# Two-layer encoder trunk: the second mixer's heads in a new order of steps, with VectorE adding the fourth sum of weight quarters

## The chip, the cores and the metric

The kernel runs on one core of a Trainium2 chip. The metric is device time in microseconds (us) for one execution of the whole program, from its start to its end.

## The reference, cut to what matters

The program is an encoder trunk of two layers on 256 rows of 2048 features, all in float32. Layer 1 mixes with differential attention, layer 2 with gated linear attention; each is followed by a squared-ReLU MLP of 8192 hidden features and has residual connections and layer norms. The change lies in the second mixer:

```python
def gla(x, w_in, w_gk2, b_gk, g_norm, w_o):
    proj = x @ w_in                       # q, k: 4 heads x 256; v, r: 4 heads x 512; z: 16
    q, k, v, r, z = jnp.split(proj, [...], axis=-1)
    log_a = jax.nn.log_sigmoid(z @ w_gk2 + b_gk) / 16
    ...                                   # b = cumsum of log_a in each chunk of 64 rows
    attn = jnp.where(causal, (q * exp(b)) @ (k * exp(-b)).T, 0)
    o = attn @ v + (terms of earlier chunks)
    o = rms_norm(o, g_norm) * silu(r)
    return o @ w_o
```

## The kernel before, in words

**Products in three parts.** TensorE multiplies in float32r. To keep float32 accuracy, each weight tile is split in two: ScalarE copies `raw` into a rounded `hi`, and VectorE subtracts, `lo = raw - hi`. Activations `X` lie ready as two such parts too. Each product is then three groups of matmuls: high part times `hi`, low part times `hi`, high part times `lo`. A weight tile is 128 partitions by 4 x 512 numbers (1 MB). `hi` has four slots, `lo` three; the semaphores `hi_ready`, `lo_ready` and `w_used` count tiles, and a slot is written again once the tile that lay there is used.

**The four heads.** After q and k of all heads (groups `G_GLA` to `G_GLA + 3`), a loop over four heads computes v and r (512 columns each, 16 blocks of 128 input features, in four "quarters" 0 to 3). Quarters 0 and 1 of v and r, for two row blocks, would be eight products; a Strassen-like scheme makes seven of them, `p0` to `p6`, from sums of weight quarters and from sums of activations (`gla_form`, forms S1 to S4, made once). Quarters 2 and 3 are plain tiles: `v2`, `v3`, `r2`, `r3`. A product is 12 matmuls, a plain tile 24. `HEAD_AT` fixes the order on TensorE: p0, p1, p3, p2, p5, p4, v2, p6, v3, r2, r3. Between them `key_pairs` makes the score maps of the head (24 small matmuls), `weigh_gla` multiplies them with v (9), and `turn_gla` transposes the output of the head before.

**Sums of weight quarters.** Four sums are needed in a head. `head_sum(h, 1)` and `head_sum(h, 2)` are made by VectorE in place in the raw slot of role 0 (for p1 and p2). The third (`head_sums(h, 3)`, for p4) and the fourth (`head_sums(h, 4)`, for p6) are transfers that accumulate, issued on GpSimd's queue: they read a quarter from HBM and add it to what lies in the slot. Each waits until the tile's last reader is through.

**What else goes on.** Of the head before: `r_total` (VectorE) ends r, `sigmoid_block` (ScalarE) and `gate_r` (VectorE) make silu(r), `gain_r` (GpSimd) multiplies by the norm's gain, `norm_gla` (VectorE) scales the output, `o_hi_gla` and `o_lo_gla` split it. Of this head: `keep` (ScalarE) copies a finished product from PSUM, so that p2, p5 and p4 can go on in its bank (`product_kept`), `r_difference` and `split_v` (VectorE) combine them. Each engine has its instructions in one written order, so that an instruction that waits holds up all behind it. SyncE issues the plain loads in written order too; the load of `v2` goes to the raw slot that held v's quarter 1 (role 3: p3's tile, and an operand of `head_sum(h, 2)`), and waits for `lo` of p3. The loads of v3, r2 and r3 wait for `lo` of p5, p4 and p6.

**Head 0.** VectorE also makes the key tensors there, `gla_k(0)` for heads 0 and 1 and `gla_k(1)` for heads 2 and 3. Both used one buffer `gla_qk`, so the k sums of group `G_GLA + 3` waited until `gla_k(0)` was done.

**After the heads.** `rows_late` is the first output group of the mixer (also used for the first mixer's).

Of the kernel before, what the change touches and what calls it, by code (L numbers as in the profile page):

```python
# [32 lines left out]
D = 2048  # L33
# [82 lines left out]
FORM_LO = {S1: 1, S2: 2, S3: 3, S4: 4}  # L116
BANK = 4
# [3 lines left out]
def build(nc, x, attn_w_qkv, attn_w_o, attn_lambda, attn_subln, gla_w_in, gla_w_gk2, gla_b_gk,  # L121
          gla_norm, gla_w_o, mlp_w1, mlp_w2, ln_g, ln_b, out):
    ctx = ExitStack()
    with ctx:
# [95 lines left out]
        gla_qk = part(3072, 2, 2, SEQ)  # L220
# [113 lines left out]
        gla4_added = sem("gla4_added")  # L334
# [53 lines left out]
        def _(sp):  # L388
# [122 lines left out]
            for h in range(GLA_HEADS):  # L511
# [3 lines left out]
                sp.wait_ge(lo_ready, at + HEAD_AT["p3"])  # L515
                load_head(h, HEAD_RAW["v2"], 2, v)
# [24 lines left out]
        def _(pool):  # L541
# [79 lines left out]
            def head_sums(h, n):  # L621

                a = HEAD_TILES * h + 4 * G_VR
                if n == 3:
                    pool.wait_ge(gla_summed, 2 * h + 1)
                    c = 2 * KEY + D + COLS * h
                    pool.dma_start(raw[:, head_slot(h, 1)], w_in[:, KPT:2 * KPT, c:c + COLS], accum_op=ALU.add
                                   ).then_inc(gla3_added, 16)
                else:
                    pool.wait_ge(lo_ready, a + HEAD_AT["p2"] + 1)  # L630
                    c = 2 * KEY + COLS * h
                    pool.dma_start(raw[:, head_slot(h, 0)], w_in[:, KPT:2 * KPT, c:c + COLS], accum_op=ALU.add
                                   ).then_inc(gla4_added, 16)
# [9 lines left out]
            def gain_r(h):  # L643
                for t in range(TB):
                    pool.wait_ge(r_gated, 2 * h + t + 1)
                    pool.tensor_tensor(silu_r[:, t, :], silu_r[:, t, :], gla_gain, ALU.mult).then_inc(r_gained, 1)

            head_sums(0, 3)
# [12 lines left out]
            gain_r(GLA_HEADS - 1)  # L661
# [12 lines left out]
        def _(pe):  # L674
# [22 lines left out]
            def rows_late(g, acts, ready, bank_free, after=None):  # L697


                for t, tiles in ((0, (0, 1, 2)), (1, (0, 1, 2)), (0, (3,)), (1, (3,))):  # L700
                    for j in tiles:
                        if j == 0:
                            pe.wait_ge(*bank_free[t])
                        if t == 0:
                            pe.wait_ge(lo_ready, 4 * g + j + 1)
                            pe.wait_ge(*ready(j))
                        acc = ps[:, 4 * t, :]
                        for k in range(KPT):
                            a = 4 * j + k
                            mm(acc, acts[:, a, 0, blk(t)], hi[:, j, k, :], a == 0, False)  # L710
                            mm(acc, acts[:, a, 0, blk(t)], lo[:, j, k, :], False, False)
                            m = mm(acc, acts[:, a, 1, blk(t)], hi[:, j, k, :], False, a == KT - 1)
# [512 lines left out]

            def head(h):
# [14 lines left out]
                pe.wait_ge(form_lo, FORMED_GLA + FORM_LO[S1])  # L1241
# [3 lines left out]
                pe.wait_ge(form_lo, FORMED_GLA + FORM_LO[S2])  # L1245
# [18 lines left out]
            for h in range(GLA_HEADS):  # L1264
# [3 lines left out]
                (0, 2): lambda: turn_gla(h, 0), (1, 0): lambda: turn_gla(h, 1)})  # L1268
# [7 lines left out]
        def _(act):  # L1276
# [356 lines left out]
            def head_hi(h, name):  # L1633
# [3 lines left out]
                if name in ("p1", "p2"):  # L1637
                    act.wait_ge(gla_summed, 2 * h + int(name[1]))
                elif name == "p4":
                    act.wait_ge(gla3_added, 16 * h + 16)  # L1640
                elif name == "p6":
                    act.wait_ge(gla4_added, 16 * h + 16)
# [43 lines left out]
            def head_squares(h):  # L1686
                act.wait_ge(go_done, h + 1)
                for t in range(TB):
# [5 lines left out]
            head_form_high(S1)  # L1694
            head_hi(0, "p1")
            for h in range(GLA_HEADS):
                if h == 0:
                    act.wait_ge(w_used, 4 * G_VR)
                    head_form_high(S3)
                    head_form_high(S2)  # L1700
                    head_form_high(S4)
                    copy_halves(G_GLA + 3, COLS_GLA + 3, 1, gla_half)
                    head_hi(0, "p3")
# [8 lines left out]
                keep(h, "p2", 0, silu_r[:, 0, :], (go_normed, 2 * h - 1) if h else (key_step, 8 * GLA_HEADS))  # L1712
                head_hi(h, "v2")
                if h:
                    o_hi_gla(h - 1, 0)
                    o_hi_gla(h - 1, 1)
                copy_pairs(h)
                head_hi(h, "p6")
                head_hi(h, "v3")
                head_hi(h, "r2")  # L1720
                head_hi(h, "r3")
                v_high(h)
                if h + 1 < GLA_HEADS:
                    head_hi(h + 1, "p0")
                    head_hi(h + 1, "p1")
                    head_squares(h)
                    head_hi(h + 1, "p3")
                else:
                    split_hi(G_GWO, 0, G_GWO - AHEAD_GWO)
                    split_hi(G_GWO, 1, G_GWO - AHEAD_GWO)  # L1730
# [877 lines left out]
```

## Time and profile before

| what | value |
|---|---|
| median of 3 runs | 2150.2 us (2144.88 to 2152.44) |
| the profiled execution | 2147.14 us |
| its span in the trace | 2145.4 us |
| TensorE busy | 2115.8 us, 99% |
| VectorE, ScalarE, GpSimd busy | 1751.6, 1195.7, 187.0 us |
| mean granted TensorE clock | 0.994 |

In the span TensorE is busy nearly throughout. Matmuls are pipelined: a 128x512 one has a duration of 0.39 us, but the next starts 0.227 us behind it, so that spacing, and not duration, tells the pace. "Idle before" is the time that an engine stood still ahead of an instruction, and the arrow names what released it.

### The profile page before, as it was taken

What the parts mean: (1) busy time and instruction counts of PE and PEld (TensorE: products, weight loads), DVE (VectorE), ACT (ScalarE), POOL (GpSimd) and SP (SyncE); (2) the same over time, 40 slices, a digit from 0 to 9 for tenths busy, and PEclk for the clock granted to TensorE, in tenths of its full rate; (3) what the DMA queues carried; (4) which work ended last, traced back from release to release, by engine and by line L of the source; (5) the groups of instructions that cost most, each with busy time, mean ns of one, the idle gap of its engine ahead of it and who ended that gap; (6) DMA issues with size and microseconds to landing.
All of it is one profiled execution on the core that took longest, in us unless ns stands there. A gap on an engine that the chain in (4) does not pass through costs nothing.

```text
span 2145.4 us, 27042 instructions
## 1 busy us (share of the span) xinstructions
PE 2115.8 (99%) x10922; PEld 1811.0 (84%) x10922; DVE 1751.6 (82%) x1489; ACT 1195.7 (56%) x1066; POOL 187.0 (9%) x155
## 2 busy tenths in 40 slices
PE   9999999999999999999999999999999999999998
PEld 8888888988888888888887777889888888888886
DVE  5555559888998998988878667698889989989887
ACT  5444445556666656656474555545566666566562
POOL 3000000300000000000110111103000000000000
PEclk9999999999999999999999999999999999999999
DMA  9445547578988988888655666775788888888884
GB/s 316 166 150 201 173 148 246 201 230 239 263 254 250 259 244 279 243 231 252 225 185 165 187 196 197 250 237 201 230 239 262 255 250 259 244 278 244 231 253 155
DMA packets 241761, 487.37 MB, mean 227 GB/s; under 512 B 7856, under 2 KB 7856, under 8 KB 240624
## 3 DMA queue, kind: packets, MB, share of 16 engines
q1 hardware_dynamic: 204928, 406.61, 53.4%
q0 software_dynamic: 36288, 78.39, 19.8%
q8 instruction: 80, 1.31, 0.2%
q10 hardware_dynamic: 432, 0.79, 0.1%
q14 instruction: 33, 0.27, 0.0%
HBM read 483.66 MB, written 2.10 MB: 226 GB/s over the span
## 4 chain that ended last, share of the span: by engine, by line
PE 93%; DVE 3%; ACT 1%; issue 1%; DMA 1%; POOL 0%; ACTq 0%; DVEq 0%
PE ps L676 57%; PE ps L1002 8%; PE ps L1000 8%; PE ps L1006 8%; PE ps L880 2%; PE ps L937 1%; PE ps L942 1%; PE ps L935 1%; PE ps L1215 1%; PE ps L1222 1%; PE ps L1217 1%; DMA raw<-in_gla_w_in_dram 1%; ACT hi L1646 1%; DVE lo L2413 1%; PE ps L747 1%
## 5 line engine op out<-in xcount | busy, mean ns | idle before, releaser
L676 PE MATMUL ps<-X,hi 128*128 128x512 f32 (+1 forms) x3008 | 697.2, 377 | 2.7 <-ACT work L1601 1.2
L676 PEld LDWEIGHTS ps<-X,hi 128*128 128x128 f32 x3008 | 549.2, 188 | 102.7 <-ACT work L1601 1.4
L1484 ACT ACTIVATE hi<-raw 128x2048 fp32r<-128x2048 f32 x196 | 372.6, 1915 | 236.3 <-DVE raw L2145 152.0
L2131 DVE TENSOR_TENSOR lo<-raw,hi 128x2048 fp32r<-128x2048 f32 x196 | 444.7, 2286 | 20.0 <-PE ps L1006 10.8
L676 PE MATMUL ps<-X,lo 128*128 128x256 f32 x2816 | 387.0, 283 | 0.0
L676 PEld LDWEIGHTS ps<-X,lo 128*128 128x128 f32 x2816 | 373.2, 191 | 12.8
L1750 DVE TENSOR_TENSOR lo<-raw,hi 128x2048 fp32r<-128x2048 f32 x104 | 237.7, 2296 | 106.7 <-ACT hi L1282 104.9
L1282 ACT ACTIVATE hi<-raw 128x2048 fp32r<-128x2048 f32 x119 | 226.3, 1914 | 157.5 <-PE ps L676 117.4
L2131 DVE TENSOR_TENSOR lo<-up_raw,hi 128x2048 fp32r<-128x2048 f32 x112 | 256.0, 2286 | 32.3 <-PE ps L676 32.3
L1468 ACT ACTIVATE hi<-up_raw 128x2048 fp32r<-128x2048 f32 x112 | 214.2, 1912 | 22.1 <-PE ps L1006 11.2
L1000 PE MATMUL ps<-hi,forms 128*128 128x512 f32 x448 | 175.3, 391 | 0.4 <-issue 0.4
L1002 PE MATMUL ps<-hi,forms 128*128 128x512 f32 x448 | 175.5, 392 | 0.0
L2156 DVE TENSOR_TENSOR res<-res,ps 128x512 f32<-128x512 f32 x196 | 131.3, 682 | 49.7 <-PE ps L1006 49.5
L2413 DVE TENSOR_TENSOR lo<-raw,hi 128x2048 fp32r<-128x2048 f32 x44 | 99.6, 2288 | 43.7 <-ACT hi L1646 43.7
L2145 DVE TENSOR_TENSOR raw<-raw 128x2048 f32<-128x2048 f32 x56 | 127.9, 2284 | 0.0
L1006 PE MATMUL ps<-lo,forms 128*128 128x512 f32 x448 | 119.7, 389 | 0.0
L1646 ACT ACTIVATE hi<-raw 128x2048 fp32r<-128x2048 f32 x44 | 82.8, 1908 | 62.4 <-DMA raw<-in_gla_w_in_dram 30.0
L1495 ACT ACTIVATE work<-ps 128x512 f32<-128x512 f32 x64 | 34.7, 595 | 133.0 <-PE ps L676 133.0
L555 POOL DMA_DIRECT2D raw<-in_mlp_w_dram x28 | 36.1, 1290 | 739.7 <-DVE raw L2145 739.7
L1006 PEld LDWEIGHTS ps<-lo,forms 128*128 128x128 f32 x448 | 84.1, 188 | 17.4
L1000 PEld LDWEIGHTS ps<-hi,forms 128*128 128x128 f32 x448 | 84.5, 189 | 15.6 <-issue 0.7
L1002 PEld LDWEIGHTS ps<-hi,forms 128*128 128x128 f32 x448 | 84.5, 189 | 15.4
(278 smaller groups left out, 2860.3 us busy)
## 6 DMA issues: line engine op xcount, KB each, us to landing
raw<-in_mlp_w_dram SPq DMA_DIRECT2D x144, 1024.0 KB, 7.9
up_raw<-in_mlp_w_dram SPq DMA_DIRECT2D x112, 1024.0 KB, 7.7
raw<-in_mlp_w_dram POOLq DMA_DIRECT2D x56, 1024.0 KB, 9.2
raw<-in_gla_w_in_dram SPq DMA_DIRECT2D x48, 1024.0 KB, 5.5
raw<-in_attn_w_qkv_dram SPq DMA_DIRECT2D x47, 1024.0 KB, 5.1
raw<-in_attn_w_o_dram SPq DMA_DIRECT2D x16, 1024.0 KB, 6.4
raw<-in_gla_w_o_dram SPq DMA_DIRECT2D x16, 1024.0 KB, 6.4
raw<-in_gla_w_in_dram POOLq DMA_DIRECT2D x8, 1024.0 KB, 9.0
```

Of the source, the lines that this page charges most:

```text
L676: return pe.matmul(o, w, m, start=start, stop=stop)
L1000: pe.matmul(acc, a_hi, hi[:, at % 4, k, :], start=start and k == 0, stop=not start, skip_group_check=not start)
L1002: pe.matmul(acc, a_lo, hi[:, at % 4, k, :], start=False, stop=not start, skip_group_check=not start)
L1006: m = pe.matmul(acc, a_hi, lo[:, at % 3, k, :], start=False, stop=k == KPT - 1 or not start, skip_group_check=not start)
L1282: act.activation(hi[:, j], raw[:, j], ACT.Copy).then_inc(hi_ready, 1)
L1468: act.activation(hi[:, U_AT[j] % 4], up_raw[j % UP_SLOTS][:, :, :], ACT.Copy).then_inc(hi_ready, 1)
L1484: act.activation(hi[:, P_AT[p] % 4], raw[:, slot], ACT.Copy).then_inc(hi_ready, 2 if p == PRODUCTS - 1 else 1)
L1750: dve.tensor_tensor(lo[:, j], raw[:, j], hi[:, j].bitcast(F32), ALU.subtract).then_inc(lo_ready, 1)
L2131: dve.tensor_tensor(lo[:, at % 3], src, hi[:, at % 4].bitcast(F32), ALU.subtract).then_inc(lo_ready, n)
L2145: dve.tensor_tensor(raw[:, a], raw[:, a], raw[:, j], ALU.add).then_inc(t_summed, 1)
L2156: dve.tensor_tensor(d, d, ps[:, BANK + bank, :], op).then_inc(res_added, 1)
L2413: dve.tensor_tensor(lo[:, n % 3], raw[:, head_slot(h, HEAD_RAW[name])], hi[:, n % 4].bitcast(F32), ALU.subtract).then_inc(lo_ready, 1)
```

## The change

Four things:
1. The fourth sum of weight quarters is made by VectorE (`head_sum(h, 3)`: the raw slot of role 0 plus that of role 3, in which v's quarter 1 still lies), not by a transfer. So v2's load, which overwrites role 3, now waits for that sum as well.
2. The written orders on TensorE, ScalarE and VectorE change. VectorE's `head_sum(h, 2)` comes right behind `lo` of p1, in the head before; ScalarE splits p3 and p2 ahead of the sigmoids; `lo` of the next head's p0 comes between `v_total` and `split_v`. On TensorE the transposes of the head before come behind p4, both together; `key_pairs` comes behind p5 (in head 0 behind p4).
3. In head 0 `gla_qk` has a second buffer, and `gla_k(1)` is moved behind the split of v2, in two halves around the split of p6.
4. v2 and `rows_late` take the matmuls on `hi` first, row block by row block, and wait for `lo` only behind them (before: `rows_late` waited for `lo` at once).

```diff
@@ sync
                 sp.wait_ge(lo_ready, at + HEAD_AT["p3"])
+                sp.wait_ge(gla_summed, 3 * h + 3)
                 load_head(h, HEAD_RAW["v2"], 2, v)
@@ gpsimd
-                    gain_r(h - 1)
-                head_sums(h, 4)
+                    gain_r(h - 1, 0)
+                    gain_r(h - 1, 1)
                 mask_pairs(h)
                 if h + 1 < GLA_HEADS:
-                    head_sums(h + 1, 3)
+                    third_sum(h + 1)
                 gla_power(h)
@@ tensor, rows_late
                         if t == 0:
-                            pe.wait_ge(lo_ready, 4 * g + j + 1)
+                            pe.wait_ge(hi_ready, 4 * g + j + 1)
...
@@ tensor, head
                 head_product(h, "p2", 0, form(S2), False)
+                pe.wait_ge(product_kept, 3 * h + 2)
+                pe.wait_ge(form_lo, FORMED_GLA + GLA_LO[S4])
+                head_product(h, "p5", 1, form(S4), False)
+                if h:
+                    key_pairs(h)
+                pe.wait_ge(product_kept, 3 * h + 3)
+                pe.wait_ge(form_lo, FORMED_GLA + GLA_LO[S3])
+                head_product(h, "p4", 0, form(S3), False)
                 if h:
                     turn_gla(h - 1, 0)
-                pe.wait_ge(product_kept, 3 * h + 2)
-                pe.wait_ge(form_lo, FORMED_GLA + FORM_LO[S4])
-                head_product(h, "p5", 1, form(S4), False)
-                if h:
                     turn_gla(h - 1, 1)
-                key_pairs(h)
-                pe.wait_ge(product_kept, 3 * h + 3)
-                head_product(h, "p4", 0, form(S3), False)
-                head_tile(h, "v2", (3, 0), False, (r_differed, h + 1))
+                else:
+                    key_pairs(h)
+                head_tile_by_rows(h, "v2", (3, 0), (r_differed, h + 1))
@@ scalar
+            head_form_high(S2)
             head_hi(0, "p1")
+            head_hi(0, "p3")
             for h in range(GLA_HEADS):
...
                 else:
+                    head_hi(h, "p2")
                     sigmoid_block(h - 1, 0)
+                    keep(h, "p0", 0, first_kept[:, :], free)
                     sigmoid_block(h - 1, 1)
-                keep(h, "p0", 0, first_kept[:, :], (go_done, h) if h else None)
-                head_hi(h, "p2")
-                keep(h, "p1", 1, second_kept, (go_done, h) if h else None)
-                head_hi(h, "p5")
+                    head_hi(h, "p5")
+                keep(h, "p1", 1, second_kept, free)
                 head_hi(h, "p4")
@@ vector, heads 1 to 3
                     r_total(h - 1, 0)
                     head_lo(h, "p3")
                     r_total(h - 1, 1)
-                    head_sum(h, 2)
                     gate_r(h - 1, 0)
                     head_lo(h, "p2")
                     gate_r(h - 1, 1)
                     head_lo(h, "p5")
+                    head_sum(h, 3)
                     norm_gla(h - 1, 0)
                     norm_gla(h - 1, 1)
                     head_lo(h, "p4")
...
                 head_lo(h, "r3")
-                split_v(h)
+                v_total(h)
                 if h + 1 < GLA_HEADS:
                     head_lo(h + 1, "p0")
+                    split_v(h)
                     head_sum(h + 1, 1)
                     head_lo(h + 1, "p1")
+                    head_sum(h + 1, 2)
                     mean_squares(h)
```

## Rows read from the trace of the kernel before

**Rows 1.** The page's busy time of the engines over the whole span
```profile
PE 2115.8 (99%) x10922; PEld 1811.0 (84%) x10922; DVE 1751.6 (82%) x1489; ACT 1195.7 (56%) x1066; POOL 187.0 (9%) x155
```

**Rows 2.** Busy time by windows, one per head; columns: PE, PEld, DVE, ACT, POOL, PEclk, DMA
```profile
1160.62:1217.22 56.60, 50.98 (x215) 41.98 (x214) 42.02 (x41) 29.02 (x29) 3.61 (x4) 0.91 0.69 194
1217.22:1269.79 52.57, 48.83 (x222) 39.79 (x221) 36.20 (x28) 27.58 (x28) 8.23 (x6) 0.97 0.68 198
1269.79:1322.48 52.69, 48.76 (x222) 39.39 (x221) 36.64 (x28) 26.64 (x24) 8.22 (x6) 0.97 0.68 198
1322.48:1375.60 53.12, 49.83 (x223) 40.50 (x222) 34.92 (x28) 29.94 (x31) 7.59 (x6) 0.94 0.75 217
```

**Rows 3.** The waits of TensorE, whole span: total us, times, longest us
```profile
PE ps L1195 <- ACT hi L1646: 9.7, 4, 3.0
PE ps L1185 <- DVE work L2476: 3.8, 3, 2.3
PE ps L1201 <- DVE lo L2413: 2.9, 2, 2.7
```

**Rows 4.** Timeline of TensorE, end of head 0: start us, us, instruction
```profile
1209.74 0.39 PE L676 MATMUL ps<-gla_v_hi,pair_hi 128*128 128x512 f32 x1
...
1211.78 0.39 PE L1215 MATMUL ps<-hi,X 128*128 128x512 f32 x1
...
1217.22 0.39 PE L1195 MATMUL ps<-hi,X 128*128 128x512 f32 x1
```

**Rows 5.** Timeline of TensorE, heads 0 and 1, where it stalls and slows
```profile
1171.89 0.47 PE L1195 MATMUL ps<-hi,gla_form 128*128 128x512 f32 x1 [2.91 <-ACT hi L1646]
...
1174.04 0.63 PE L1195 MATMUL ps<-hi,gla_form 128*128 128x512 f32 x1
...
1181.00 1.19 PE L1201 MATMUL ps<-lo,gla_form 128*128 128x512 f32 x4 [2.71 <-DVE lo L2413]
...
1232.58 0.66 PE L1185 MATMUL ps<-ident,work 128*128 128x128 f32 x4 [2.27 <-DVE work L2476]
...
1237.84 2.79 PE L676 MATMUL ps<-G 128*128 128x64 f32 x24
1240.44 0.48 PE L1195 MATMUL ps<-hi,gla_form 128*128 128x512 f32 x1
```

**Rows 6.** Timeline of VectorE, head 0 and the start of head 1
```profile
1149.47 0.69 DVE L2393 TENSOR_TENSOR G<-G,work 128x512 f32<-128x512 f32 x1
...
1154.09 2.28 DVE L2413 TENSOR_TENSOR lo<-raw,hi 128x2048 fp32r<-128x2048 f32 x1
...
1192.03 6.69 DVE L2413 TENSOR_TENSOR lo<-raw,hi 128x2048 fp32r<-128x2048 f32 x3
...
1220.83 2.28 DVE L2421 TENSOR_TENSOR raw<-raw 128x2048 f32<-128x2048 f32 x1
```

**Rows 7.** Timeline of ScalarE: three splits in head 0, table load in head 1
```profile
1188.14 5.51 ACT L1646 ACTIVATE hi<-raw 128x2048 fp32r<-128x2048 f32 x3
...
1217.90 1.28 ACT L1668 ACT_TABLE_LOAD   x1
```

**Rows 8.** All GpSimd gains (line 646): duration ns min/median/max
```profile
L646 POOL TENSOR_TENSOR work<-work x8: 1266/2272/3272, 1223.9 to 1383.7; 128x512 f32<-128x512 f32 x8
```

**Rows 9.** Timelines of GpSimd and VectorE behind head 3: a gain beside two VectorE operations
```profile
1379.76 3.27 POOL L646 TENSOR_TENSOR work<-work 128x512 f32<-128x512 f32 x1 [7.35 <-DVE work L2469]
...
1381.80 1.78 DVE L2469 TENSOR_TENSOR work<-work 128x512 f32<-128x512 f32 x1
```

**Rows 10.** Transfers, from issue to landing: SyncE's plain loads (line 501)
```profile
DMA to landing us min/median/max: 4.9/5.6/10.8
```

**Rows 11.** The same for GpSimd's fourth sum (line 632)
```profile
DMA to landing us min/median/max: 8.4/11.9/12.5
```

**Rows 12.** Timeline of TensorE, head 2: a short stall and the matmul behind it
```profile
1286.22 0.66 PE L1185 MATMUL ps<-ident,work 128*128 128x128 f32 x4 [1.31 <-DVE work L2476]
...
1286.94 0.39 PE L1197 MATMUL ps<-hi,gla_form 128*128 128x512 f32 x1
```

More of the change, by code:

```diff
@@ L116 @@
 FORM_LO = {S1: 1, S2: 2, S3: 3, S4: 4}
+GLA_HI = {S1: 1, S2: 2, S3: 3, S4: 4}
+GLA_LO = {S1: 1, S2: 2, S4: 3, S3: 4}
 BANK = 4
@@ L641, in mask_pairs, with gain_r @@
                                    pattern=[[0, 2], [1, P]], channel_multiplier=-1).then_inc(pairs_masked, 1)
[L643 to L648, printed above, removed]
+            def gain_r(h, t):
+                pool.wait_ge(r_gated, 2 * h + t + 1)
+                pool.tensor_tensor(silu_r[:, t, :], silu_r[:, t, :], gla_gain, ALU.mult).then_inc(r_gained, 1)
+            third_sum(0)
             pool.wait_ge(form_lo, FORMED_GLA + 4)
@@ L710, in rows_late @@
                             mm(acc, acts[:, a, 0, blk(t)], hi[:, j, k, :], a == 0, False)
-                            mm(acc, acts[:, a, 0, blk(t)], lo[:, j, k, :], False, False)
-                            m = mm(acc, acts[:, a, 1, blk(t)], hi[:, j, k, :], False, a == KT - 1)
+                            mm(acc, acts[:, a, 1, blk(t)], hi[:, j, k, :], False, False)
+                        if t == 0:
+                            pe.wait_ge(lo_ready, 4 * g + j + 1)
+                        for k in range(KPT):
+                            a = 4 * j + k
+                            m = mm(acc, acts[:, a, 0, blk(t)], lo[:, j, k, :], False, a == KT - 1)
                         if t == 1:
@@ L1224, in head_tile, with head_tile_by_rows @@
                 m.then_inc(w_used, 1)
+            def head_tile_by_rows(h, name, banks, second_free):
+                n = HEAD_TILES * h + HEAD_AT[name]
+                a = KPT * int(name[1])
+                pe.wait_ge(hi_ready, 4 * G_VR + n + 1)
+                for t in range(TB):
+                    if t:
+                        pe.wait_ge(*second_free)
+                    for k in range(KPT):
+                        for part_of_x in range(2):
+                            pe.matmul(ps[:, banks[t], :], X[:, a + k, part_of_x, blk(t)], hi[:, n % 4, k, :], start=False,
+                                      stop=True, skip_group_check=True)
+                    if t == 0:
+                        pe.wait_ge(lo_ready, 4 * G_VR + n + 1)
+                    for k in range(KPT):
+                        m = pe.matmul(ps[:, banks[t], :], X[:, a + k, 0, blk(t)], lo[:, n % 3, k, :], start=False,
+                                      stop=True, skip_group_check=True)
+                m.then_inc(w_used, 1)
             def head(h):
@@ L2374, in gla_k_sums, with gla_k @@
                     b = 4 * (u % 2) + 2 * s
-                    dve.tensor_tensor(gla_qk[:, s], ps[:, b:b + 2, 0:SEQ], gla_half[:, s], ALU.add
+                    dve.tensor_tensor(gla_qk[u][:, s], ps[:, b:b + 2, 0:SEQ], gla_half[:, s], ALU.add
                                       ).then_inc(halves_added, 1)
-            def gla_k(u):
+            def gla_k(u, only=(0, 1)):
                 n = COLS_GLA + 2 + u
                 dve.wait_ge(decays_ready, 5)
-                for s in range(2):
+                for s in only:
                     h = 2 * u + s
@@ L2516, in _ @@
             gla_form_lo(S1)
-            gla_k(0)
             head_lo(0, "p0")
             head_sum(0, 1)
+            gla_form_lo(S2)
+            gla_k(0)
             head_lo(0, "p1")
+            head_sum(0, 2)
             for h in range(GLA_HEADS):
                 if h == 0:
-                    gla_form_lo(S2)
-                    gla_k_sums(1)
                     head_lo(0, "p3")
-                    head_sum(0, 2)
+                    head_lo(0, "p2")
+                    gla_form_lo(S4)
                     gla_form_lo(S3)
-                    gla_form_lo(S4)
-                    head_lo(0, "p2")
-                    gla_k(1)
+                    head_sum(0, 3)
                     head_lo(0, "p5")
                     head_lo(0, "p4")
+                    gla_k_sums(1)
+                    head_lo(0, "v2")
+                    r_difference(0)
+                    gla_k(1, (0,))
+                    head_lo(0, "p6")
+                    gla_k(1, (1,))
+                    head_lo(0, "v3")
+                    pairs_low(0)
+                    head_lo(0, "r2")
                 else:
```

83 lines of the change are left out of this document (42 added, 41 removed).

## The prediction

> **What bounds the kernel now.** I read the busy time of the page first: TensorE is at work 99% of the span [rows 1], so only what makes it stand or run slowly can be won. Then its waits over the whole program: nearly all that matter lie at three lines of the four heads, 9.7 + 3.8 + 2.9 = 16.4 us [rows 3]. Then windows, one for each head: 56.60, 52.57, 52.69 and, up to the first matmul of the output group, about 52.9 us, at a granted clock of 0.91 to 0.97 [rows 2]. That clock is the second loss.
>
> The least that a head can take comes from a stretch without stalls [rows 4]: a plain tile takes 5.44 us (1211.78 to 1217.22), so a product with half as many matmuls 2.72, and `weigh_gla` 2.04. `key_pairs` takes 2.60 (1237.84 to 1240.44) [rows 5], the two transposes about 0.9. So a head needs 7 x 2.72 + 4 x 5.44 + 2.04 + 2.60 = 45.4 us, and 46.3 with the transposes (heads 1 to 3). Above that lie 11.2, 6.3, 6.4 and 6.6 us: 30.5 us in all, the most that the change can bring here. The stalls are 16.4 of it; the rest is slow matmuls of 0.63 us, in place of 0.39, behind them [rows 5].
>
> **Why it stalls.** Before, VectorE makes `head_sum(h, 2)` 3.6 us into the head (1220.83 to 1223.11 in head 1, [rows 6]), ScalarE splits p2 only behind that and a sigmoid, and TensorE waits. In head 0 `gla_k(1)` (4.6 us, as `gla_k(0)` from 1149.47 to 1154.09, [rows 6]) stands ahead of the splits of p5 and p4: the 2.71 us stall. In heads 1 to 3 the transposes wait for `norm_gla` (2.27 us at the longest) [rows 5].
>
> **The prices.** A split or a sum on VectorE takes 2.28 us alone and 2.20 in a row (6.69 for three) [rows 6], a 512-wide operation 0.6; a split on ScalarE 1.8 in a row and 1.9 alone (5.51 for three, [rows 7]); a plain load 5.6 us to landing [rows 10]. T is a head's start on TensorE.
>
> **Part 1, head 0.** VectorE now does `lo` p0 at 1149.5, sum 1, form S2, `gla_k(0)` to 1159.1, `lo` p1 to 1161.4, sum 2 to 1163.6, `lo` p3, `lo` p2 to 1168.0. TensorE wants p2 at 1168.8, and its `lo` 1.8 us later: the 2.91 stall goes. Forms S4 and S3, sum 3 to 1171.4, `lo` p5 to 1173.6: p5 starts at 1171.5 and wants `lo` at 1173.3, so 0.25 us are lost. `lo` p4 (1175.8) is in time. v2's load goes at 1171.4, lands at 1177.0, `hi` at 1179.0, ahead of 1179.9 where TensorE comes to it. The halves of `gla_k(1)` (2.3 us each) delay `lo` of p6 and v3 to 1186.4 and 1190.9, needed at 1187.1 and 1191.6: hidden, with 0.7 us to spare. If that cover went, each later microsecond would be one of TensorE's. What comes late next is `weigh_gla`: r3's load waits for `lo` p6, so it lands at 1192.0; `hi`, `lo`, `v_total`, the next head's `lo` p0 (now ahead of `split_v`: 2.2 us that before did not stand there) and `split_v` end at 1200.3; TensorE is there at 1198.9: 1.4 us. Head 0 then takes 45.4 + 0.25 + 1.4 = 47.1 us, 9.5 less.
>
> **Part 2, heads 1 to 3.** `head_sum(h, 2)` ends about T + 0.6 (T + 1.2 in head 1), `hi` p2 at T + 2.6, far ahead of T + 8.2: that stall (9.7 us in all four heads, 3.0 at the longest, [rows 3]) goes. The transposes are wanted at T + 18.9 and the norms end before T + 16: that stall goes too. The new critical chain hangs on sum 3, since v2's load now waits for it, and SyncE's loads of v3 and r2 queue behind it. `r_total(0)`, `lo` p3, `r_total(1)`, `gate_r(0)`, `lo` p2, `gate_r(1)`, `lo` p5, sum 3: with the sigmoid between, sum 3 ends at T + 12.0 (12.9 in head 1, whose first sigmoid has a table load of 1.28 us ahead, [rows 7]).
>
> That is if nobody disturbs VectorE. The eight gains on GpSimd take from 1.27 us, with VectorE at rest, to 3.27, started beside a split [rows 8]. In the one place where a VectorE operation with both inputs in SBUF follows, it was 1.78 us in place of the usual 0.7, while the gain ran its 3.27 us [rows 9]. In the new order `gate_r(1)` stands so behind `lo` p2 and sum 3 behind `lo` p5, each with a gain waiting. I price each at the measured 1.1 us: 2.2 us, sum 3 at T + 14.2 (15.1 in head 1). The bounds: 0, since the other gains delayed nobody, and 2 x 1.3.
>
> The Trainium skill has a rule for this ("SBUF — State Buffer", on the port pair that VectorE and GpSimd share): it is an exclusive lock, and a VectorE operation with two SBUF inputs and a GpSimd operation that reads SBUF block each other for a whole instruction. It speaks against this change, since it puts two such operations in the chain on which the load hangs. By that rule the price is the 1.1 us twice; the row of 1.78 us agrees.
>
> So v2 lands at T + 19.8, `hi` is ready at T + 21.7 (22.7 in head 1). TensorE comes to it at 8.16 + 2.72 + 2.72 + 2.60 + 2.72 + 0.9 = T + 19.8, in head 1 at T + 20.5, since `norm_gla` and `lo` p4 are late by 0.25 + 0.45 there. Stall: 1.9 us (head 1: 2.25), then 0.45 for `lo` of v2 (2.25 us behind `hi`, of which 1.8 are covered by the matmuls on `hi`), and 0.2 at `weigh_gla`. Heads 1 to 3 take 46.3 + 3.4, 46.3 + 2.6 and 46.3 + 2.6: 2.9, 3.8 and 4.0 us less.
>
> **Part 3, the transfer.** The fourth sum no longer takes 1.3 us of GpSimd's queue and 1 MB of traffic. Its landing of 8.4 to 12.5 us [rows 11] held ScalarE up at p6, but TensorE never waited there: nothing by itself. VectorE has 2.2 us more per head, within its 42 of 56.6 and 36 of 52.6 us busy [rows 2]; their price is in the chain above.
>
> **Part 4, `rows_late`.** Same matmuls, a later wait: two stalls of together 0.7 us behind head 3 go. The transposes there move back by one tile; the norms end before them, and nothing is due until the fourth tiles. In the first mixer I see no stall to win. Between 0 and 1 us; I take 0.7.
>
> **The clock.** A stall of 1.31 us was followed by matmuls at the full 2.4 GHz pace (0.39 us) [rows 12], those of 2.91 and 2.71 by some at 1.2 GHz (0.63 us) [rows 5]. The new stalls are of the first kind but in head 1 (2.25 + 0.45): I take 1 us for that, between 0 and 2 in each head.
>
> **Sum.** 9.5 + 2.9 + 3.8 + 4.0 + 0.7 - 1 = 19.9 us off the profiled execution's 2147.1 us: 2127.2. The median of the runs shown is 3.1 us above that execution; from there it would be 2130.3. I predict 2128.
>
> **Rivals.**
> A. GpSimd's gains do not hold VectorE up (only one of eight did). Sum 3 ends 2.2 us sooner, v2's stall falls to 0 to 0.65 us. The heads take 47.1, 47.6, 46.7 and 46.7: 27.4 us less, 2119.7 to 2122.8: 2121.
> B. The new orders leave other steps late, of which I have the slack only to some 0.7 us: `lo` of p6 and v3 in head 0, `weigh_gla` in each, loads at up to 7 us. One to two more microseconds for each of 4 heads, with the clock falling behind them: 8 to 13 us less than before, about 2139.
> C. Slower. One mechanism: v2's load hangs on sum 3 and everything of the head behind it. For: the longest plain load took 10.8 us [rows 10]. At that, each of heads 1 to 3 stalls 5.2 us more, above the 2.9 us from which rows show slow matmuls, some 14 of them at 0.2 us each: 3 x (5.2 + 2.8) = 24 us, 4 more than is won: 2152. It decides from about 9.5 us of landing. Against: that is the maximum of 32, and the median is 5.6.
> D. It doesn't do what it says: that TensorE's waits are for another engine than the order suggests. Against: each of the three waits has the written order ahead of it. It would give about 2148.
>
> **How the numbers follow.** Forecast 0.52, A 0.22, B 0.15, C 0.05, D 0.06. The range reaches from A with all stalls gone (30.5 us less, 2117) to B's middle, 2140; outside are some 0.15. A measurement of this kernel tells about 0.3%, 6.4 us, from no change. Faster by more: 0.89 (forecast, A, B); within: 0.06 (D); slower: 0.05 (C).
>
> **What would show it.** Of the changed kernel: TensorE without a wait ahead of p2 and the transposes; one of 1 to 2.5 us at the first matmul of v2 in heads 1 to 3, released by ScalarE's `hi`, and this by the load; `gate_r(1)` and sum 3 at about 1.8 and 3.4 us; a short wait at `weigh_gla` for VectorE's `split_v`; heads of 47, 50, 49 and 49 us at a clock above 0.97. If v2's matmuls don't wait, A holds. If the wait is at `lo` of p6 or v3, it is B. Head 0 at over 50 us would show my count of its VectorE chain wrong.

## The result, and the profile after

The changed kernel takes 2128.09 us (median of 4 runs, 2127.86 to 2130.45); the kernel before, on the same chip, 2149.92 us (2144.88 to 2152.44). The ratio is 0.9904, with a 95% interval of 0.9885 to 0.9923: faster by about 1%. The profiled execution took 2127.86 us, with a span of 2126.1 us, 19.3 less than the span of before.

The page's busy times, as [rows 1] before:

```profile
PE 2105.4 (99%) x10922; PEld 1804.8 (85%) x10922; DVE 1765.5 (83%) x1493; ACT 1195.6 (56%) x1066; POOL 193.2 (9%) x151
```

TensorE has 10.4 us less to show, though its matmuls are the same 10922: fewer of them run slowly. VectorE has 13.9 us more, of which four sums of 2.3 us are the work that the change gives it. The windows of the four heads, as [rows 2] (us, PE, PEld, DVE, ACT, POOL, PEclk, DMA):

```profile
1160.59:1208.78 48.19, 46.19 (x216) 38.01 (x214) 43.08 (x41) 27.29 (x26) 2.35 (x3) 1.00 0.64 199
1208.78:1259.30 50.52, 47.80 (x222) 38.85 (x221) 41.44 (x29) 28.57 (x27) 10.57 (x5) 1.00 0.60 186
1259.30:1310.04 50.74, 48.64 (x222) 39.97 (x221) 41.42 (x29) 27.16 (x26) 10.64 (x5) 0.97 0.61 188
1310.04:1359.02 48.98, 47.30 (x222) 38.85 (x221) 36.16 (x27) 27.17 (x26) 9.99 (x5) 1.00 0.61 204
```

The heads were 56.60, 52.57, 52.69 and 52.91 us, 214.8 together, and are 198.4 now. Below, "the four heads" is this sum, always from the first matmul of p0 to that of the next head or of the output group. It holds nothing of the rest of the program, so it tells more than the whole time does. TensorE's waits, as [rows 3] (total us, times, longest us):

```profile
PE ps L1235 <- ACT hi L1667: 5.1, 3, 2.1
...
PE ps L671 <- DVE gla_v_lo L2532: 1.5, 1, 1.5
...
PE ps L671 <- issue: 0.8, 1, 0.8
...
PE ps L1200 <- DVE lo L2440: 0.5, 1, 0.5
...
PE ps L1240 <- DVE lo L2440: 0.4, 2, 0.2
...
PE ps L1194 <- ACT work L1682: 0.2, 1, 0.2
```

The three waits of before, 16.4 us, are gone (products, line 1194, and transposes, line 1184, now wait for next to nothing). New are one at the first matmul of v2 in heads 1 to 3 (line 1235), and two at `weigh_gla` (line 671, in heads 0 and 1). With the four short ones these rows make 8.5 us. Where the first of them comes from stands on VectorE in head 1 (start us, us, instruction):

```profile
1214.44 2.28 DVE L2440 TENSOR_TENSOR lo<-raw,hi 128x2048 fp32r<-128x2048 f32 x1
1216.64 1.78 DVE L2498 TENSOR_TENSOR work<-work 128x512 f32<-128x512 f32 x1
1218.35 2.28 DVE L2440 TENSOR_TENSOR lo<-raw,hi 128x2048 fp32r<-128x2048 f32 x1
1220.55 3.38 DVE L2448 TENSOR_TENSOR raw<-raw 128x2048 f32<-128x2048 f32 x1
```

These are `lo` p2, `gate_r(1)`, `lo` p5 and sum 3. The second and the fourth take 1.78 and 3.38 us where the same operation takes 0.68 and 2.28 elsewhere. GpSimd in the same stretch:

```profile
1214.67 3.20 POOL L640 TENSOR_TENSOR work<-work 128x512 f32<-128x512 f32 x1 [3.87 <-DVE work L2498]
1218.50 3.28 POOL L640 TENSOR_TENSOR work<-work 128x512 f32<-128x512 f32 x1 [0.63 <-DVE work L2498]
1231.57 2.05 POOL L635 TENSOR_SCALAR_AFFINE_SELECT work<-work 128x256 f32<-128x256 f32 x1 [9.79 <-ACT work L1698]
```

Each gain starts just behind the start of a split, and ends 1.2 us inside the VectorE operation that follows. Sum 3 ends at 1223.93, and only then goes v2's load; ScalarE gets it 5.2 us later, TensorE after that:

```profile
1229.11 1.91 ACT L1667 ACTIVATE hi<-raw 128x2048 fp32r<-128x2048 f32 x1 [3.83 <-DMA raw<-in_gla_w_in_dram]
```

```profile
1231.07 2.11 PE L1235 MATMUL ps<-hi,X 128*128 128x512 f32 x8 [1.50 <-ACT hi L1667]
1233.40 1.19 PE L1240 MATMUL ps<-lo,X 128*128 128x512 f32 x4 [0.22 <-DVE lo L2440]
...
1251.70 0.47 PE L671 MATMUL ps<-gla_v_hi,pair_hi 128*128 128x512 f32 x1 [0.78 <-issue]
```

In head 2 the same wait is longer, and the eight matmuls behind it take 3.61 us, where eight behind a wait of 1.47 us in head 3 took 2.11, and eight without a wait take 1.98. It is the only head whose granted clock is not 1.00:

```profile
1281.71 3.61 PE L1235 MATMUL ps<-hi,X 128*128 128x512 f32 x8 [2.10 <-ACT hi L1667]
```

**Where the 19.3 us of span went.** 16.3 in the heads. 1.2 in the output group behind them, before (first row) and after:

```profile
1375.39:1399.36 23.97, 23.32 (x105) 18.66 (x104) 20.69 (x16) 9.91 (x8) 5.76 (x4) 1.00 0.69 252
```

```profile
1359.02:1381.76 22.74, 22.74 (x106) 18.81 (x105) 18.41 (x14) 9.68 (x8) 5.76 (x4) 1.00 0.68 243
```

And 1.7 in a place that the change does not touch, the last six matmuls of the program, before and after:

```profile
2137.57 4.54 PE L676 MATMUL ps<-work,end_minus 128*128 128x512 f32 x6 [1.29 <-DVE end_minus L2011]
```

```profile
2119.96 2.84 PE L671 MATMUL ps<-work,end_minus 128*128 128x512 f32 x6 [1.29 <-DVE end_minus L2039]
```

The wait ahead of them is the same 1.29 us; the matmuls run at the slow pace in one profile and at the full one in the other. They do so in the profiles of the experiments too, now this way and now that, and the start of the program, around its first transposes, varies likewise by 0.8 to 1.7 us. So a whole time carries some 3 us that is not the change's doing. The kernel before scatters more: over all the experiments its executions took 2141.7 to 2153.0 us, in the experiments' own rounds those above 2149 at a mean granted clock of 0.993 or 0.994 and the shortest at 0.997. It has one trace only, so where in the program this lies is not shown.

### The profile page after: what moved, and what is told of

It is laid out like the page before. It is cut to its first block, busy times and chain, and to the rows that moved or that the text cites. A ratio compares the mean times of both kernels' runs of the same rounds, so it can differ in the third digit from the quotient of the medians.

```text
span 2126.1 us, 27052 instructions
## 1 busy us (share of the span) xinstructions
PE 2105.4 (99%) x10922; PEld 1804.8 (85%) x10922; DVE 1765.5 (83%) x1493; ACT 1195.6 (56%) x1066; POOL 193.2 (9%) x151
## 4 chain that ended last, share of the span: by engine, by line
PE 92%; DVE 4%; DMA 2%; ACT 1%; issue 1%; POOL 1%; DVEq 0%; SPq 0%; POOLq 0%; ACTq 0%
PE ps L671 57%; PE ps L1001 8%; PE ps L999 8%; PE ps L1005 8%; PE ps L879 2%; PE ps L934 1%; PE ps L936 1%; PE ps L941 1%; DMA raw<-in_gla_w_in_dram 1%; DVE lo L2440 1%; DVE raw L2448 1%; PE ps L1221 1%; PE ps L1214 1%; PE ps L1216 1%; PE ps L746 1%
## 5 line engine op out<-in xcount | busy, mean ns | idle before, releaser
L2159 DVE TENSOR_TENSOR lo<-raw,hi 128x2048 fp32r<-128x2048 f32 x196 | 444.7, 2287 | 19.6 <-PE ps L1005 10.4
```

The source lines that it names most:

```text
L2159: dve.tensor_tensor(lo[:, at % 3], src, hi[:, at % 4].bitcast(F32), ALU.subtract).then_inc(lo_ready, n)
```

## Experiments

All are edits of the changed kernel, but one, which edits the kernel before. "Us" is the median of at least 4 runs, the ratio is to the kernel before on the same chip (whose own median lay between 2145.8 and 2151.2 us, so the heads are compared first). Head 0 has the same steps in six of these kernels (changed, no gain, sum 3 earlier, sum 2 late, transposes early, `rows_late`) and took 47.6 to 48.3 us there: less than that, 0.7 us, is no difference between two heads.

| kernel | us | ratio, 95% interval | heads 0 to 3, us | sum |
|---|---|---|---|---|
| before | 2149.9 | 1 | 56.6, 52.6, 52.7, 52.9 | 214.8 |
| changed | 2128.1 | 0.9904 [0.9885, 0.9923] | 48.2, 50.5, 50.7, 49.0 | 198.4 |
| no gain on GpSimd | 2122.7 | 0.9876 [0.9849, 0.9903] | 47.8, 48.6, 48.3, 46.8 | 191.4 |
| fourth sum by transfer | 2119.4 | 0.9857 [0.9829, 0.9884] | 47.4, 46.5, 46.5, 46.5 | 186.8 |
| sum 3 earlier | 2120.0 | 0.9863 [0.9836, 0.9890] | 47.6, 47.4, 46.5, 46.5 | 188.0 |
| `split_v` first | 2131.6 | 0.9916 [0.9889, 0.9943] | 46.5, 51.6, 50.7, 50.8 | 199.6 |
| before, with the sum alone | 2162.8 | 1.0072 [1.0052, 1.0093] | 60.5, 56.7, 55.8, 56.8 | 229.8 |
| sum 2 late | 2142.4 | 0.9977 [0.9966, 0.9988] | 47.7, 55.3, 54.1, 52.9 | 210.0 |
| keys ahead in head 0 | 2137.7 | 0.9956 [0.9938, 0.9973] | 56.8, 50.7, 50.4, 49.1 | 207.0 |
| transposes early | 2135.1 | 0.9947 [0.9927, 0.9968] | 47.8, 53.0, 51.4, 52.9 | 205.1 |
| three orders combined | 2126.9 | 0.9912 [0.9893, 0.9931] | 46.4, 53.1, 48.1, 48.1 | 195.8 |
| transfer, combined | 2118.3 | 0.9869 [0.9851, 0.9887] | 45.6, 48.1, 46.6, 46.5 | 186.8 |
| `rows_late` waits for `lo` | 2131.0 | 0.9927 [0.9909, 0.9945] | 48.3, 50.7, 50.2, 49.0 | 198.2 |

### The gains taken off GpSimd

```diff
-pool.tensor_tensor(silu_r[:, t, :], silu_r[:, t, :], gla_gain, ALU.mult).then_inc(r_gained, 1)
+pool.sem_inc(r_gained, 1)
```

> The changed kernel with GpSimd's eight multiplications by the norm's gain left out (r is not multiplied by the gain; the semaphore is only counted up), so the output lacks that factor. Theory L (the gains hold VectorE up, and with it sum 3 and v2's load): gate_r(1) goes back from 1.78 to 0.68 us and sum 3 from 3.38 to 2.28, sum 3 ends 2.2 us sooner in heads 1 to 3, TensorE's waits at v2 (1.50, 2.10, 1.47 us) fall below 0.5 each and the slow matmuls in head 2 go: 5 to 8 us faster than the changed kernel, about 2121. Rival Q (v2's load is late for a reason of its own, SyncE's queue or the transfer): sum 3 may end sooner but the load doesn't land sooner, 2127 to 2129.

The same two VectorE operations in head 1:

```profile
1216.29 0.68 DVE L2498 TENSOR_TENSOR work<-work 128x512 f32<-128x512 f32 x1
1216.89 2.28 DVE L2440 TENSOR_TENSOR lo<-raw,hi 128x2048 fp32r<-128x2048 f32 x1
1219.09 2.28 DVE L2448 TENSOR_TENSOR raw<-raw 128x2048 f32<-128x2048 f32 x1
```

Both 1.1 us are gone, so the gains cause them. TensorE no longer waits for v2's `hi`, and the heads are 7.0 us shorter: the prediction had the lock's price right, from one row. The whole time is near what rival A gave, 2121, but its heads are not: they sum to 191.4 us, and A had 188.1. Waits of 1.02 and 1.21 us at `weigh_gla` are left in heads 1 and 2, which A did not have.

### The fourth sum given back to the transfer, with the new order kept

```diff
 # sync, ahead of v2's load
-                sp.wait_ge(gla_summed, 3 * h + 3)
 # gpsimd
                     gain_r(h - 1, 0)
-                    gain_r(h - 1, 1)
+                fourth_sum(h)
+                if h:
+                    gain_r(h - 1, 1)
 # vector
-                    head_sum(0, 3)
...
-                    head_sum(h, 3)
```

`fourth_sum(h)` is the accumulating transfer; it waits for `lo` of p2, the last reader of its slot.

> The changed kernel, with the fourth sum made by the accumulating transfer again (issued by GpSimd between the two gains, once lo of p2 is done) and v2's load waiting for lo of p3 alone. Theory (the new order of steps is what won the time, and the sum on VectorE costs some of it, as v2's load hangs on it): no wait at v2, lo of p5 in head 0 in time, heads 1 to 3 at 46.5 to 48 us, 6 to 9 us faster than the changed kernel, about 2120. Rival (the transfer was itself a part of the loss of before): its landing of 8.4 to 12.5 us makes TensorE wait at p6, and the time is 2128 or above.

```profile
1209.46:1255.95 46.49, 46.49 (x222) 38.99 (x221) 39.18 (x28) 28.66 (x27) 10.54 (x6) 1.00 0.81 232
1255.95:1302.41 46.46, 46.46 (x222) 38.98 (x221) 38.12 (x28) 27.50 (x26) 9.62 (x6) 1.00 0.78 227
```

These windows are heads 1 and 2: the time is TensorE's busy time, to the hundredth. Nothing waits in heads 1 to 3; in head 0 a wait of 1.52 us at `weigh_gla` is left. So the change has two halves of opposite sign. The new order alone takes 27.9 us off the heads (214.8 to 186.8); the sum on VectorE, with v2's load waiting for it, gives 11.6 us of it back (186.8 to 198.4, or 8.7 us between the medians).

### Sum 3 ahead of `lo` of p5 and of `gate_r(1)`

```diff
                     head_lo(h, "p2")
-                    gate_r(h - 1, 1)
-                    head_lo(h, "p5")
                     head_sum(h, 3)
+                    head_lo(h, "p5")
+                    gate_r(h - 1, 1)
                     norm_gla(h - 1, 0)
-                    norm_gla(h - 1, 1)
                     head_lo(h, "p4")
+                    norm_gla(h - 1, 1)
```

> The changed kernel with VectorE's order in heads 1 to 3 altered: lo p2, sum 3, lo p5, gate_r(1), norm(0), lo p4, norm(1), so that sum 3 has one operation less and one lock less ahead of it. Theory (v2's load hangs on the end of sum 3): sum 3 ends about 4 us sooner, v2 lands in time, the three waits at v2 go; lo of p5 is at most 0.5 us late. 5 to 7 us faster than the changed kernel, about 2122. Rival (moving it only shifts the wait): TensorE waits 1 us or more at lo of p5 or at p4 in each head, and the time is 2126 to 2129.

```profile
1216.28 3.20 DVE L2448 TENSOR_TENSOR raw<-raw 128x2048 f32<-128x2048 f32 x1
```

Sum 3 is held up here too (3.20 us), but it starts 4.3 us sooner (3.7 counted from the head's start), so the load and v2 are in time and TensorE does not wait for them. The time is 8.1 us below the changed kernel's, a little more than was expected. So it is less the sum on VectorE that costs than its place: at 188.0 us the heads are within 1.2 us of those with the transfer. The edit also swaps `gate_r(1)` and `lo` of p5, and `norm_gla(1)` and `lo` of p4; no run tells these moves apart.

### `split_v` ahead of the next head's `lo` of p0

```diff
                 v_total(h)
                 if h + 1 < GLA_HEADS:
-                    head_lo(h + 1, "p0")
                     split_v(h)
+                    head_lo(h + 1, "p0")
                     head_sum(h + 1, 1)
```

> One part of the change undone: split_v goes back ahead of lo of the next head's p0 (v_total, split_v, lo p0). Theory (that move made the waits at weigh_gla, 1.46 us in head 0 and 0.78 in head 1, and p0 had room to spare): both waits go, 2 to 2.5 us faster than the changed kernel, about 2125.7. Rival (p0, sum 1 and p1 come late instead): waits at lo of p0 or at p1 of 1 us and more, 2128 or above.

This one missed: 5.9 us more than expected. Both waits at `weigh_gla` went, and head 0 became 1.7 us shorter (48.19 to 46.46). But in head 1 others took their place (TensorE's waits):

```profile
PE ps L1235 <- ACT hi L1667: 4.5, 3, 1.6
PE ps L1194 <- DVE work L2480: 2.7, 3, 1.2
...
PE ps L1194 <- ACT work L1682: 1.5, 3, 0.8
```

TensorE now waits at the next head's products, three times at p1 for `r_total`, three times for a kept product. I read it as a loop that runs through VectorE and the loads, beside TensorE: `lo` of p6 lets r3's load go; `lo` of r3, `v_total`, `split_v`, sum 1, `lo` p1 and sum 2 of the next head follow on VectorE; then `r_total`, `gate_r`, sum 3; v2's load; `lo` v2, `lo` p6. Take one step of it, the sums 1 for heads 1 and 2, in the changed kernel:

```profile
1200.94 2.28 DVE L2448 TENSOR_TENSOR raw<-raw 128x2048 f32<-128x2048 f32 x1
...
1251.52 2.28 DVE L2448 TENSOR_TENSOR raw<-raw 128x2048 f32<-128x2048 f32 x1
```

Every wait of VectorE between these two is ended by ScalarE. Three of the four above 1 us (at `lo` of p1, v2 and r3; the fourth, 1.25 us, is at `lo` of p6):

```profile
1205.21 2.29 DVE L2440 TENSOR_TENSOR lo<-raw,hi 128x2048 fp32r<-128x2048 f32 x1 [1.98 <-ACT hi L1667]
...
1231.05 2.29 DVE L2440 TENSOR_TENSOR lo<-raw,hi 128x2048 fp32r<-128x2048 f32 x1 [3.61 <-ACT hi L1667]
...
1245.31 2.29 DVE L2440 TENSOR_TENSOR lo<-raw,hi 128x2048 fp32r<-128x2048 f32 x1 [1.40 <-ACT hi L1667]
```

ScalarE's own waits there are ended by VectorE, by a load or by the mask, and none in this stretch by TensorE. The same holds in this kernel (1202.45 to 1253.51). With the transfer it does not hold: there TensorE ends a wait of VectorE at `v_total` (1.06 us in head 1).

So in these two kernels the loop runs by itself, once in 50.6 and 51.1 us, against 46.5 us of matmuls in a head, and TensorE waits for it. (The distance alone would not show that: where engines wait for each other, each has the length of the head between two of its steps, whichever leads.) While the loop is longer than TensorE's own work, a wait taken away at one of TensorE's steps comes back at another. With sum 3 earlier the step is at 1200.40, 1247.32 and 1293.57: 46.9 and then 46.3 us, and behind head 1 TensorE waits no more. That this loop also explains the kernels below rests on waits that move, and is less sure.

Of the 3.8 us by which the span with `split_v` first is above that of the changed kernel, 1.2 lie in the heads, 1.0 ahead of them and 1.7 in the last six matmuls, told of above.

### The kernel before, with the sum on VectorE and nothing else

```diff
 # edit of the kernel before
                 sp.wait_ge(lo_ready, at + HEAD_AT["p3"])
+                sp.wait_ge(gla_summed, 3 * h + 3)
...
-                head_sums(h, 4)
...
                     head_lo(h, "p5")
+                    head_sum(h, 3)
                     norm_gla(h - 1, 0)
```

> The kernel before, with the second part of the title alone: the fourth sum is made by VectorE (behind lo of p2 in head 0, behind lo of p5 in heads 1 to 3) and v2's load waits for it; all orders stay as before. Theory (the sum on VectorE is a cost, the order of steps is the gain): norm_gla comes 2.2 us later, and 1.1 more by the gain on GpSimd, so TensorE waits some 3 us more at the transposes of heads 1 to 3 and 2.2 more at lo of p5 in head 0, with slow matmuls behind: 10 to 14 us slower than before, about 2162. Rival (the transfer was part of the loss of before): faster than before or equal, 2146 to 2151.

```profile
PE ps L1185 <- DVE work L2476: 16.6, 3, 5.5
PE ps L1195 <- ACT hi L1646: 6.9, 4, 2.9
PE ps L1201 <- DVE lo L2413: 5.1, 2, 5.0
```

Of [rows 3], the wait at the transposes grew from 3.8 to 16.6 us and that for `lo` from 2.9 to 5.1. In the old order the norms stand behind sum 3, and the transposes come right behind p2: there is no room for 2.3 us more, nor for the 1.07 by which a gain stretches it (3.35 us in head 1). Slower than before by 0.72%: by itself the sum on VectorE is a loss of 15 us in the heads and by the ratio, 17 between the medians, and so somewhat more than the 10 to 14 expected.

### Each new place taken back

Three kernels each move one step of the changed kernel to where it was before: sum 2 behind `r_total(1)`; `gla_k(1)` ahead of the splits of p5 and p4; the transposes behind p2 and p5.

```diff
 # vector
                     head_lo(h + 1, "p1")
-                    head_sum(h + 1, 2)
...
                     r_total(h - 1, 1)
+                    head_sum(h, 2)
```

> The changed kernel with one move undone: in heads 1 to 3 sum 2 goes back behind r_total(1). Theory (that move is what frees p2 and the chain behind it): sum 2 ends near T + 5.8 in place of T + 0.6, hi of p2 is just in time, but the sigmoid and gate_r behind it, and so sum 3 and v2's load, come 4 us later: TensorE waits about 5 us in place of 1.5 to 2 at v2, at 1.2 GHz behind it. 12 to 18 us slower than the changed kernel, about 2143. Rival (only p2's own wait matters, and that has 5 us of room): within 2 us of the changed kernel.

```profile
PE ps L1235 <- ACT hi L1667: 4.8, 3, 1.7
PE ps L1200 <- DVE lo L2440: 4.1, 7, 0.9
PE ps L1194 <- ACT first_kept L1682: 3.1, 3, 2.0
PE ps L1194 <- ACT work L1682: 2.5, 3, 0.8
```

The size came as expected (11.6 us in the heads, 14.3 between the medians), but not the place. In head 1 sum 3 starts 4.8 us later in the head, about as expected: ScalarE's `hi` of p2 waits for sum 2, the sigmoids and the copy of p0 stand behind it, and VectorE waits 3.92 us for the first sigmoid at `gate_r(0)`. But v2's `hi` is not waited for longer than in the changed kernel (4.8 us in three heads, 5.1 there), since TensorE has been held up before it: 3.1 us ahead of p2, for that copy, and 3.6 and 2.3 us more than there at `lo` and at p4.

```diff
 # vector, head 0
                     head_sum(0, 3)
+                    gla_k_sums(1)
+                    gla_k(1)
                     head_lo(0, "p5")
```

> The changed kernel with the whole of gla_k(1) and its sums back ahead of lo p5 in head 0. Theory: lo of p5 comes 5.8 us later, TensorE waits 6 us there in place of 0.55 and runs some ten matmuls at 1.2 GHz; the wait of 1.5 us at weigh_gla of head 0 goes, since nothing holds lo p6 any more. 4 to 7 us slower than the changed kernel, about 2133.5. Rival (head 0 is held by the loads, not by VectorE): no change.

```profile
PE ps L1200 <- DVE lo L2440: 6.3, 1, 6.3
...
PE ps L671 <- DVE gla_v_lo L2532: 1.4, 1, 1.4
```

The 6.3 us at `lo` of p5 came as expected, but head 0 is 8.6 us longer and the median 9.6 us, where 4 to 7 were expected. The wait at `weigh_gla` was expected to go with the halves of `gla_k(1)`, and did not (1.4 us, 1.46 in the changed kernel). So it is not the halves that make it. The changed kernel's trace agrees: ScalarE has `hi` of p6 ready at 1184.0 us, and `lo` of p6 starts at 1184.27, so the half ahead of it held it up by 0.3 us at most. The run with `split_v` first shows that without the split of p0 ahead of it the wait is gone.

```diff
 # tensor
                 head_product(h, "p2", 0, form(S2), False)
+                if h:
+                    turn_gla(h - 1, 0)
...
                 head_product(h, "p5", 1, form(S4), False)
                 if h:
+                    turn_gla(h - 1, 1)
                     key_pairs(h)
```

> The changed kernel with TensorE's transposes back behind p2 and p5 in heads 1 to 3. Theory: they wait for norm_gla, which ends near T + 15, at T + 10.9: 4 us of wait in each of three heads and matmuls at 1.2 GHz behind; part of it is won back at v2, whose load lands at the same time as before. 8 to 14 us slower than the changed kernel, about 2139. Rival (the loop is closed by VectorE and the loads, so that TensorE's waits only move): within 3 us of the changed kernel.

```profile
PE ps L1184 <- DVE work L2505: 11.6, 3, 4.8
```

11.6 us of waits at the transposes, but only 6.6 more in the heads and 7.0 between the medians, where 8 to 14 were expected: the 5.1 us at v2 went, since TensorE, held up ahead of it, now finds v2 ready. The loss is real, so the rival (waits only move) is not the whole of it either.

### Combining the better places

The first takes the two orders above (sum 3 earlier, `split_v` first) and puts `r_total(0)` ahead of sum 2; the second does the same with the transfer, without sum 3.

```diff
                     head_lo(h + 1, "p1")
-                    head_sum(h + 1, 2)
                     mean_squares(h)
+                    r_total(h, 0)
+                    head_sum(h + 1, 2)
```

> The changed kernel with three moves together: sum 3 early (as in e3_sum3_early), split_v ahead of lo of the next p0 (as in e4_split_v_first), and r_total(0) ahead of sum 2, so that p1 doesn't wait for it. Theory (with the loop through sum 3 slack, a wait that is taken away at weigh_gla is won; in e4_split_v_first it only moved to p1): the waits at weigh_gla and p1 are both gone, the one at lo of p5 in heads 0 and 1 (0.55 and 0.65) stays: 1 to 1.5 us faster than e3_sum3_early, about 2118.7. Rival (the wait moves again, as in e4_split_v_first): equal to e3_sum3_early or slower, 2120 to 2123.

This missed by 8.2 us. `r_total` needs the end of r3 on TensorE, and so does now sum 2 behind it; VectorE stands idle (between heads 1 and 2):

```profile
1261.90 0.69 DVE L2480 TENSOR_TENSOR work<-ps,work 128x512 f32<-128x512 f32 x1 [1.88 <-PE ps L1221]
1262.51 2.28 DVE L2448 TENSOR_TENSOR raw<-raw 128x2048 f32<-128x2048 f32 x1
```

With sum 3 still to come, that is too late for `lo` of p5, where TensorE waits 2.5, 1.4 and 1.4 us; in head 1 slow matmuls follow (53.05 us, at a granted clock of 0.94). I had moved a step that depends on TensorE into a chain that was meant to run ahead of it.

> The same with the fourth sum by transfer: e2_fourth_by_transfer with split_v ahead of lo of the next p0 and r_total(0) ahead of sum 2. Theory: its only wait in the heads, 1.52 us at weigh_gla of head 0, goes: 1 to 2 us faster than e2_fourth_by_transfer, about 2118. Rival: the wait moves to p1 or p2 of head 1, 2119.5 or above.

2118.3 us is the lowest median of all, 9.8 us under the changed kernel's (7.5 by the ratios). Head 0 has no wait left (45.59 us), but the wait moved, as the rival had it: head 1 now waits 0.16 and 0.89 us at `lo` of p2 and of p5 and takes 48.1 us, 46.5 with the transfer alone. The heads sum to the same 186.8 us, so the two orders won nothing on top of the transfer. The runs of these two and of "sum 3 earlier" (2116.9 to 2120.7) all lie below every run of the changed kernel.

### `rows_late` waits for `lo` again

```diff
 # tensor, rows_late
-                            pe.wait_ge(hi_ready, 4 * g + j + 1)
+                            pe.wait_ge(lo_ready, 4 * g + j + 1)
```

> The changed kernel with rows_late waiting for lo ahead of the matmuls on hi again (their order otherwise as changed). Theory: the two waits of 0.27 and 0.39 us behind head 3 come back, 0.7 to 1.3 us; within 2 us of the changed kernel, 2128 to 2130. Rival (rows_late of the first mixer gains or loses as well): more than 2 us away from it.

```profile
PE ps L671 <- DVE lo L1778: 0.7, 2, 0.4
```

Two waits of 0.7 us together came back, as priced. The median is 2.9 us above the changed kernel, outside the 2 us expected, and the span 3.6. Of that 1.2 lies in this group (23.96 us to the first matmul of the next, 22.74 in the changed kernel); the heads are the same. 0.9 is there already 20 us into the program, is still 0.9 when the first mixer is over, and 1.7 is in the last six matmuls. So the first mixer's `rows_late`, the rival, neither gains nor loses, and this part of the change is worth 1.2 us.

## Why the prediction was right, and where it was not

2128.09 us against 2128, but errors cancel in that, and so close a hit is luck. The spans fell by 19.3 us, for which the working had 19.9; the medians fell by 21.8, since the profiled execution of before took 2.8 us less than the median of runs that lie 7.6 us apart. And 2128 was chosen between 2127.2 and 2130.3, which follow from the one and from the other.

**The chain was right.** The waits ahead of p2, at `lo` of p5 and at the transposes went. The one that takes their place is at v2 in heads 1 to 3, released by ScalarE's `hi`, and this by the load behind sum 3. In head 1 sum 3 ended at T + 15.15 us (15.1 predicted), v2's `hi` at T + 22.2 (22.7). In head 2 they were at T + 14.65 and T + 22.35 (14.2 and 21.7).

**The lock was right,** and it is the step that I was least sure of: 1.78 and 3.38 us, where 1.8 and 3.4 stood. In the Trainium skill, "SBUF — State Buffer", section "SBUF: two separate sides", says just this: a VectorE operation with two SBUF inputs and a GpSimd one that reads SBUF block each other for a whole instruction. The trace agrees in heads 1 to 3 at both operations, and without the gains (first experiment) both prices are zero.

**The heads were mis-sized.** 19.2 us were to come from them, with 1 off for the clock; 16.3 came.

| head | predicted | measured | what differs |
|---|---|---|---|
| 0 | 47.1 | 48.2 | `lo` of p5 0.55 late, not 0.25; the rest below |
| 1 | 49.7 | 50.5 | v2 1.50, not 2.25; `weigh_gla` 0.78, not 0.2 |
| 2 | 48.9 | 50.7 | slow matmuls behind v2's wait, 1.6 us |
| 3 | 48.9 | 49.0 | |

Three terms are behind this. First, the bare head: 45.59 and 46.5 us in the kernels that do not wait, where 45.4 and 46.3 stood; 0.8 us in four heads. Second, a stall costs more than its "idle": the row counts from the end of a matmul, 0.39 us behind its start, while the next would have started 0.227 us behind it. That is 0.16 us more for each, with four stalls in head 1, and the first matmul behind a stall costs another 0.1 (0.34 us to the next one). Third, the mask: `mask_pairs` on GpSimd started half a microsecond behind a VectorE split (1231.57 against 1231.05) and took 2.05 us. In the kernel before it took 0.41:

```profile
1241.33 0.41 POOL L640 TENSOR_SCALAR_AFFINE_SELECT work<-work 128x256 f32<-128x256 f32 x1 [7.10 <-ACT work L1677]
```

With it the pair tile that ScalarE makes came late:

```profile
1233.65 0.53 ACT L1700 ACTIVATE pair_hi<-work 128x384 fp32r<-128x384 f32 x1 [2.25 <-POOL work L635]
```

ScalarE splits p6 only behind that, and `lo` of p6 lets r3's load go, so `weigh_gla` waits longer. The prediction priced the lock for VectorE alone, on two operations, and forgot that the same lock holds GpSimd up, and what waits for GpSimd. This last step, from mask to wait, is read from the timelines; no run took the mask away, and it can't be all: with sum 3 earlier the mask took 2.05 us as well, and TensorE did not wait at `weigh_gla` in heads 1 to 3. A small slip besides: the prediction's own terms for head 1 (0.7 us late, 2.2 to `hi`, 0.45 and 0.2) add to 3.55 us, where it put 3.4.

**The clock** was priced at 1 us for the four heads. It was 1.6 us, all in head 2 behind a wait of 2.10 us, and not in head 1, where it was looked for; behind 1.50 and 1.47 us in heads 1 and 3 the matmuls ran at the full pace.

**What made up for it:** `rows_late`, 1.2 in place of 0.7, and the 1.7 us at the program's end, which were no part of the forecast. Without these last, the gain would have been 17.6 us, and the working 2.3 us too low.

**The rivals.** A: its condition was false. In the kernel in which it holds the time is near A's (2122.7 against 2121), with heads 3.3 us longer than A's: again errors that cancel. B: no wait at `lo` of p6 or v3; 0.6 us at `weigh_gla` in head 1 is all of it. C: v2's load took 5.2 us, not 9.5. D: the waits were what the order suggested.

**A reason that fell.** For head 0 the prediction had the wait at `weigh_gla` (1.4 us, measured 1.46) from the halves of `gla_k(1)` and from the split of p0 ahead of `split_v`. Moving the halves away changed nothing; swapping the other two took it away. And that the sum fits within VectorE's 42 of 56.6 us busy was the wrong thing to look at: its busy share is not what the sum costs, its place in a loop is. Part 3 called the transfer's removal nothing by itself, and its price in the chain 2 us or so per head; taken by itself in the old order it is a loss of 15 us, and in the new one of 9 to 12.

## What to carry to other kernels

Where a change reorders steps and also moves work from a queue to an engine, price the two apart; here they were worth minus 28 and plus 12 us, and keeping the transfer, or moving the new sum two places forward, gives a kernel 8 to 10 us faster than the change as made. When a wait that you remove comes back at another step, look for a loop through several engines and loads. Follow the waits from one of its steps to the same step of the next round: if none of them is ended by the engine that seems to be the limit, the loop sets the pace (50.6 us here, with 46.5 of matmuls), and it is the loop that has to be shortened, not a wait. And when GpSimd and VectorE work on SBUF side by side, ask of each GpSimd operation which VectorE one it will overlap, and who waits for either.

## What the runs showed of the hardware

The lock worked both ways, and on two kinds of GpSimd operation: a gain of 1.27 us takes 3.2 to 3.3 beside a split, a select of 0.41 takes 2.05, and the VectorE operation that follows a held gain pays 1.1 us (0.68 to 1.78, 2.28 to 3.38). VectorE does not pay during the split that was already running, only in the operation behind it, and where that one reads PSUM it did not pay: behind the split of v2, with the mask running to 1233.62, `r_difference`, which reads PSUM, started at 1233.26 and took its usual 0.68 us. And the pace of TensorE behind a wait of 1.3 us is not one thing: the last six matmuls of the program, behind the same 1.29 us, took 2.84 us in one profile and 4.54 in another, with the code there unchanged.
